# Expert weight pieces loaded as whole contiguous megabytes, with the activations transposed in strides to match

## The reference

```
def expert_block(args):
    tok, e = args
    xb = x_pad[tok]
    hb = jax.nn.silu(xb @ w1[e]) * (xb @ w3[e])
    return hb @ w2[e]
```

## Time and profile before

| | us |
|---|---|
| median of 3 runs | 1959.67 (1955.29 to 1959.69) |
| the profiled execution | 1964.04 |
| its span, first to last instruction | 1962.5 |

### The profile page before, as it was taken

How to read it: one execution, slowest core, us unless ns; L and a number is a source line. 1 busy time by engine, 2 the same in 40 slices (tenths; PEclk the granted TensorE clock), 3 DMA queues, 4 the chain that set the end, 5 groups by cost and what they waited for, 6 DMA issues and landing times. The chain is left out here.

```text
span 1962.5 us, 23223 instructions
## 1 busy us (share of the span) xinstructions
PE 1738.7 (89%) x8639; PEld 1375.7 (70%) x8639; DVE 1042.5 (53%) x1123; ACT 846.8 (43%) x862; POOL 128.9 (7%) x170
## 2 busy tenths in 40 slices
PE   4999999999999999988869898569999999999980
PEld 3788888879977878767758798346666666666650
DVE  4343434342205013277764421468888888888866
ACT  5243434331212121155541202237777777777751
POOL 2100000000000000011110000010000000000005
PEclk9999999999999999999999999869999999999995
DMA  5722222222332232644433310859999999999927
GB/s 175 196 94 89 92 90 91 80 90 104 129 118 75 85 110 99 229 152 172 171 111 128 128 55 28 290 195 368 380 376 374 380 376 379 375 375 380 379 83 267
DMA packets 196202, 385.96 MB, mean 197 GB/s; under 512 B 11440, under 2 KB 70904, under 8 KB 192064
## 3 DMA queue, kind: packets, MB, share of 16 engines
q1 hardware_dynamic: 184064, 343.16, 48.9%
q0 software_dynamic: 8384, 29.63, 5.3%
q10 hardware_dynamic: 3712, 12.62, 1.7%
HBM read 317.95 MB, written 67.42 MB: 196 GB/s over the span
## 5 line engine op out<-in xcount | busy, mean ns | idle before, releaser
L1470 DVE TENSOR_TENSOR e_l<-e_raw,e_h 128x2048 fp32r<-128x2048 f32 x192 | 439.5, 2291 | 107.8 <-ACT e_h L1464 105.8
L1464 ACT ACTIVATE e_h<-e_raw 128x2048 fp32r<-128x2048 f32 x192 | 364.6, 1916 | 75.4 <-PE ps L1486 49.4
L193 PE MATMUL ps<-uh,w_h 128*128 128x512 f32 x1024 | 318.2, 392 | 21.5 <-DVE ul L834 13.6
L193 PE MATMUL ps<-ul,w_h 128*128 128x512 f32 x1024 | 317.1, 391 | 0.0
L193 PE MATMUL ps<-uh,w_l 128*128 128x512 f32 x1024 | 316.6, 391 | 0.0
L177 DVE TENSOR_TENSOR w_l<-w_raw,w_h 128x2048 fp32r<-128x2048 f32 x40 | 91.6, 2291 | 361.9 <-ACT w_h L173 361.9
L193 PEld LDWEIGHTS ps<-uh,w_h 128*128 128x128 f32 x1024 | 192.9, 189 | 63.6 <-issue 22.4
L1486 PE MATMUL ps<-e_h,e_xth 128*96 128x512 f32 x512 | 204.9, 400 | 27.3 <-DVE e_l L1470 25.4
L193 PEld LDWEIGHTS ps<-ul,w_h 128*128 128x128 f32 x1024 | 193.4, 189 | 40.6
L193 PEld LDWEIGHTS ps<-uh,w_l 128*128 128x128 f32 x1024 | 193.2, 189 | 40.5
L1486 PE MATMUL ps<-e_h,e_xtl 128*96 128x512 f32 x512 | 202.7, 396 | 0.0
(11 more groups left out here) (246 smaller groups left out, 2167.7 us busy)
## 6 DMA issues: line engine op xcount, KB each, us to landing
e_raw<-w_exp_gate SPq DMA_DIRECT2D x64, 1024.0 KB, 8.6
e_raw<-w_exp_up SPq DMA_DIRECT2D x64, 1024.0 KB, 10.0
e_raw<-w_exp_down SPq DMA_DIRECT2D x64, 1024.0 KB, 10.1
w_raw<-w_in SPq DMA_DIRECT2D x28, 1024.0 KB, 5.5
qk_d<-qk SPq DMA_DIRECT2D x16, 1024.0 KB, 4.1
at_qk<-qk_d SPq DMA_DIRECT2D x8, 2048.0 KB, 8.8
y_d<-e_y ACTq DMA_DIRECT2D x32, 384.0 KB, 6.4
y_d<-zeros POOLq DMA_DIRECT2D x22, 384.0 KB, 11.0
```

The costliest lines, as they stand in the source:

```text
L193: mm = pe.matmul(ps[:, h * HALF:(h + 1) * HALF], w[:, k, :], u[:, k, h * HALF:(h + 1) * HALF], start=first, stop=last)
L1464: act.activation(self.e_h[m % SPLIT][:, :, :], self.e_raw[slot][:, :, :], ACT.Copy).then_inc(self.e_hi[m % SPLIT], 1)
L1470: dve.tensor_tensor(self.e_l[slot][:, :, :], self.e_raw[slot][:, :, :], self.e_h[m % SPLIT][:, :, :].bitcast(F32), ALU.subtract).then_inc( ...
```

## The change

A piece is now one contiguous megabyte of HBM. For gate and up, lane p takes the four consecutive rows 4p to 4p+3 of the half's 512 rows, 8 KB in one run (`RUN = 4`). For down, a half is now 256 rows of all 1024 columns, and lane p takes two consecutive rows, also 8 KB (`DOWN_RUN = 2`). Chunk k of the contraction therefore holds rows in a stride, and the transposes must deliver the matching columns: `turn_x` reads every fourth column of `xg`, `turn_h` every second column of the hidden rows (`lanes_of`). As a down half now holds half of the contraction and all output columns, the new `down_products` walks two chunks, three products each, and both halves of the output columns for each product.

```diff
+RUN, DOWN_RUN = 4, 2
...
-        w = self.ins["w_exp_" + kind][0][e].rearrange("(k p) n -> p k n", p=P)
-        src = w[:, :, half * HALF:(half + 1) * HALF] if kind == "down" else w[:, 4 * half:4 * half + 4, :]
+        run = DOWN_RUN if kind == "down" else RUN
+        lanes = self.ins["w_exp_" + kind][0][e].rearrange("(k p r) n -> p k (r n)", p=P, r=run)
+        n = lanes.shape[1] // 2
         slot, _ = self.raw_slot(piece)
-        eng.dma_start(self.e_raw[slot][:, :, :], src).then_inc(self.e_in[slot], 16)
+        eng.dma_start(self.e_raw[slot][:, :, :].rearrange("p (k r) n -> p k (r n)", k=n), lanes[:, n * half:n * half + n, :])\
+            .then_inc(self.e_in[slot], 16)
+
+    def lanes_of(self, row, chunk, run):
+        k, r = chunk // run, chunk % run
+        return row[:, k * P * run:(k + 1) * P * run].rearrange("t (p r) -> t r p", r=run)[:, r, :]
...
+    def down_products(self, pe, ps, ht_h, ht_l, piece, half):
+        j, b, m = piece
+        slot, _ = self.raw_slot(piece)
+        pe.wait_ge(self.e_lo[m % SPLIT], 2 * j + m // SPLIT + 1)
+        w_h, w_l = self.e_h[m % SPLIT], self.e_l[slot]
+        for k in range(2):
+            at = 2 * half + k
+            for x, w, first, last in ((ht_h, w_h, at == 0, False), (ht_h, w_l, False, False), (ht_l, w_h, False, at == 3)):
+                for c in range(2):
+                    mm = pe.matmul(ps[:, c * HALF:(c + 1) * HALF], x[:, at, :], w[:, 2 * k + c, :], start=first, stop=last)
+        mm.then_inc(self.e_used[m % SPLIT], 1)
...
-                mm = pe.transpose(ps_x[:, k, :], xg[b][:, k * P:(k + 1) * P], ident)
+                mm = pe.transpose(ps_x[:, k, :], k_.lanes_of(xg[b][:, :], k, RUN), ident)
...
-                mm = pe.transpose(ps_h[:, k, :], hid[:, k * P:(k + 1) * P], ident)
+                mm = pe.transpose(ps_h[:, k, :], k_.lanes_of(hid[:, :], k, DOWN_RUN), ident)
...
-            k_.piece_products(pe, ps_y[:, half * HALF:(half + 1) * HALF], ht_h, ht_l, piece, True, True)
+            k_.down_products(pe, ps_y, ht_h, ht_l, piece, half)
```

## The result

The changed kernel takes 1972.12 us as the median of 4 runs (1967.72 to 1973.91), the one before 1959.68 (4 runs, 1955.29 to 1962.65). The ratio is 1.0059 with an interval of 1.0035 to 1.0082: 12.4 us slower, where no change was forecast. The time lies inside the range of 1954 to 1973, near its upper end.

The account below looks back on a forecast made before the run. It took PE, not the transfers, to bound the experts' stage. Loads 0, route -0.5, down 0 and transposes 0 took the profiled 1964.04 us to 1963.5, or about 1959 against the median 1959.67; range 1954 to 1973.

Parts of the forecast that it names:

- The step on the transposes: turn_x and turn_h in the experts: strided stationary loads cost 0, with 20 of 82 ns spare; ends up to 42.5 us.
- Rival 1: Experts' transposes: strided loads at half speed, 1970 or 1975 us; chance 0.27 near factor two, 0.10 for more or both strides.
- Loads and queue: Experts' weight loads: 8 KB runs land perhaps 1 to 2 us sooner, worth 0; SP's queue still waits for PE.
- Stores in route: route: stores of xn_d behind two gate pieces in SP's queue go sooner, -0.5 us, ends 0 and -0.7.
- Down products: Experts' down: the same 768 matmuls in a new order, 0 us, with -4.2 as one end.
- rival 2: Experts' down: pairing speeds matmul steps from 0.233 to 0.2275 us, total 1955 us; chance 0.07.
- The gap does not absorb it: Experts: PE time added between its resumption and the end of down is paid once an expert, 32 times.
- Rival 3: Experts: transfers were the limit, so faster ones close PE's gap, 25.4 us at most, down to 1934; chance 0.06.

Follow-up runs that it names:

- e3: Kernel before with only gate and up in 8 KB runs and turn_x strided, down and turn_h as before: 1969.33 us (1.0047).
- e4: Kernel before with only down in 8 KB runs, its new product order and turn_h strided: 1964.92 us (1.0022).
- e10: Kernel before, reordered: ACT converts the next gate piece before the output copy, silu earlier, DVE writes hidden rows between gate pieces: 1938.16 us (0.9879).
- e13: Order of e10 with down loaded as whole 4 KB rows and the new down products, no transpose strided: 1930.40 us (0.9828).

## Why the prediction was wrong

*What failed.* The step on the transposes, "I take nothing". It measured 120 - 82 = 38 ns for each of 384 transposes, 14.6 us before anything is taken off, and 13.8 by the period. The argument was that 20 of the 82 ns are spare. The load grew by far more, from 140 to 218 ns. The likeliest value was taken from rows in which nothing was strided, and these say nothing on what a stride does. The slack itself was sized too low: at every fourth, second and eighth float (the last in a single run) the load grew by 78, 76 and 66 ns and the step by 38, 38 and 29, so by these lengths 37 to 40 ns of growth did not show. The prediction had worked out a load at twice as 124 ns, and 120 is what the steps show. That it came so near is in part luck, since the load's own length grew by a factor of 1.56.

*The second float.* Rival 1 had every fourth float alone at 1970 and both strides at 1975. The second is what happened, at 1972.1. It had the smaller chance, in line with the Trainium skill, "Advanced Engine Details and Errata", section SBUF Cachelines: two hits on a line of 16 bytes should suffice for full speed. For every fourth float the runs agree with the page (218 ns instead of 140). For every second they contradict it: 216 ns with two hits on each line, and every eighth float, a new line each time, is a little cheaper at 206. The measurement decides.

*Loads and queue.* Held. 7.3 KB a packet, 8.6 us to landing where "8 to 9" stood, no wait for weights before or after, and the change without strides at 0.9984.

*Stores in route.* The stall shrank by 0.86 us and PE's gap of 0.68 there went, for -0.5 in the sum. A time for it can't be told: from the first load of weights to the first gather were 63.7 us before and 63.2 after, and over all the kernels that leave the order of the rows as it was this lies between 63.1 and 64.4.

*Down products.* Held at 0. The median step is 0.232 us a matmul, 0.233 before, so rival 2's 0.2275 comes from the 128 stationary columns of its rows or another difference there.

*The gap does not absorb it.* Held. 25.4 us became 25.2, and the period grew by the 0.43 us added to PE. `turn_h` and `turn_x` both lie in the stretch of which the prediction spoke, from PE's resumption behind the gap to the end of down, and both were paid (e3, e4).

*Rival 3, transfers as the limit.* Wrong for this kernel. It becomes right once the gap is closed, and then only when the lead is used up: e10's transfers move 379 GB/s from 1400 us on, with and without anyone waiting, and its period goes from 17.84 to 18.65 us when ACT starts to wait for weights. Its 1934 us assumed that faster transfers would close the gap. Only the order closed it, and transfers then set how much of it was kept.

## What to carry to other kernels

A layout that makes transfers longer is paid for by whoever must read or write in the stride; price that on the engine which sets the pace before the transfers, and when no row shows the operation, don't let contiguous rows choose its value. Look for the longest run that needs no stride (here 4 KB, a whole row) before going on to the longest of all. A load's speed is worth something only once the consumer waits for it: close the gap in the order first, then measure the change again, because a change that lost 12 us in one order came out even in the other. And look at the steps one by one and not only at their mean: buffers filled beforehand can hide a transfer that is too slow for most of a stage, and the comparison then depends on how long the stage is.

## What the runs showed of the hardware that was not expected

- A stationary load of 128 float32 columns takes TensorE 140 ns when they are contiguous and 216, 218 and 206 ns at every second, fourth and eighth float. Behind an identity of 96 columns the steps are 82 ns, then 120, 120 and 111.
- VectorE pays as well: `e_hid` in 256 floats, read in order and written 128 floats apart in turn, takes 612 ns, and 512 contiguous floats take 676. How much of it is the stride and how much the shorter instruction was not measured apart; 256 contiguous floats would take about 418 ns by the estimate above.
- The experts' transfers stopped at 379 GB/s in runs of 2 KB (e10, the same while the lead shrank and while ACT waited) and at 384 with a third of the bytes in runs of 4 KB (e13, the lead shrinking). They reached 392 and 396 GB/s in runs of 8 KB with nobody waiting, so their own limit lies higher and was not found.
